# Sums of squares of the head outputs: added up per kind before TensorE sums them over partitions

## The reference, cut to what matters

```python
z = h @ w_in                         # q, k, v of both kinds, gate path, forget logits
o_sb = stick_breaking_attention(...) # (1024, 512)
o_fx = forgetting_attention(...)     # (1024, 512)
y = concatenate([rmsnorm(o_sb, g_grp[:512]), rmsnorm(o_fx, g_grp[512:])])   # one mean square per row and kind
y = y * silu(g_path)
x = x + (1 + gate) * (y @ w_out)
return rmsnorm(x, g_final)
```

## Time and profile before

| | before |
|---|---|
| median of 3 runs | 832.3 us (832.14 to 835.11) |
| profiled execution, first to last instruction | 828.7 us |
| around the span (median less span) | 3.6 us |
| mean granted TensorE clock | 0.973 |
| PE busy | 720.7 us (87%) |
| DVE busy | 490.9 us (59%) |
| ACT busy | 408.4 us (49%) |
| POOL busy | 390.7 us (47%) |

### The profile page before, as it was taken

The page is one execution under the profiler, slowest core; times in us unless marked ns, Lnnn a source line. Parts: engine busy times, 40 slices in busy tenths (PEclk is TensorE's granted clock), DMA queues, the critical chain, the costliest instruction groups (busy, mean ns, idle before and its releaser), DMA issues.

```text
span 828.7 us, 10998 instructions
## 1 busy us (share of the span) xinstructions
PE 720.7 (87%) x3936; PEld 604.4 (73%) x3936; DVE 490.9 (59%) x993; ACT 408.4 (49%) x846; POOL 390.7 (47%) x325
## 2 busy tenths in 40 slices
PE   0257965989999999999989989998899899999996
PEld 0146754768887887888777878887788788788884
DVE  1486663776564567756634676565447765545565
ACT  4027333576457555554645555555556465623132
POOL 2244422535866563467476644665556465221100
PEclk9988997999999999999989999999999999999998
DMA  6553332104245431133342411244432308894223
GB/s 185 183 200 148 129 100 40 35 22 86 98 102 138 108 103 26 26 91 102 88 136 57 102 26 26 77 128 127 152 94 67 85 25 304 243 311 166 68 90 128
DMA packets 64390, 91.57 MB, mean 111 GB/s; under 512 B 5448, under 2 KB 39880, under 8 KB 63824
## 3 DMA queue, kind: packets, MB, share of 16 engines
q1 hardware_dynamic: 57216, 72.17, 30.4%
q0 software_dynamic: 5376, 14.68, 5.6%
q10 hardware_dynamic: 1744, 4.02, 1.2%
HBM read 67.23 MB, written 23.63 MB: 110 GB/s over the span
## 4 chain that ended last, share of the span: by engine, by line
PE 34%; DMA 21%; POOL 19%; issue 9%; DVE 9%; ACT 6%; SPq 1%; DVEq 0%; POOLq 0%; ACTq 0%
DMA w_raw<-in_w_in 15%; PE psum L1376 10%; POOL w_lo L540 6%; DMA work<-in_w_ada_t 5%; PE psum L1290 4%; PE psum L1291 4%; PE psum L1295 4%; PE psum L1364 4%; DVE work L1037 3%; PE psum L1342 3%; POOL w_hi L534 3%; POOL work L554 2%; POOL work L608 2%; DVE stacks L1005 2%; POOL work L614 2%
## 5 line engine op out<-in xcount | busy, mean ns | idle before, releaser
L1290 PE MATMUL psum<-h_hi,w_hi 128*128 128x512 f32 x496 | 209.6, 423 | 23.9 <-POOL h_lo L591 13.5
L1295 PE MATMUL psum<-h_hi,w_lo 128*128 128x512 f32 x496 | 197.6, 398 | 0.0
L1291 PE MATMUL psum<-h_lo,w_hi 128*128 128x512 f32 x496 | 197.2, 398 | 0.0
L800 ACT ACTIVATE pt_hi<-psum 128x512 fp32r<-128x512 f32 (+1 forms) x192 | 87.5, 490 | 140.5 <-PE psum L1342 137.3
L1097 DVE TENSOR_TENSOR pt_lo<-psum,pt_hi 128x512 fp32r<-128x512 f32 (+1 forms) x192 | 100.6, 551 | 84.4 <-ACT pt_hi L800 83.4
L608 POOL TENSOR_TENSOR work<-work 128x127 f32<-128x127 f32 (+3 forms) x64 | 77.4, 1211 | 152.2 <-DVE work L1037 152.2
L1290 PEld LDWEIGHTS psum<-h_hi,w_hi 128*128 128x128 f32 x496 | 96.0, 193 | 43.6 <-issue 16.2
L1037 DVE TENSOR_TENSOR_SCAN work<-work 128x128 f32<-128x128 f32 (+3 forms) x64 | 104.1, 1627 | 32.5 <-ACT work L768 32.4
L1342 PE MATMUL psum<-ident,work 128*128 128x128 f32 x576 | 88.8, 282 | 29.9 <-POOL work L614 16.0
L1295 PEld LDWEIGHTS psum<-h_hi,w_lo 128*128 128x128 f32 x496 | 95.5, 192 | 22.2
L1291 PEld LDWEIGHTS psum<-h_lo,w_hi 128*128 128x128 f32 x496 | 96.1, 194 | 16.6
(11 more groups left out here) (141 smaller groups left out, 1291.5 us busy)
## 6 DMA issues: line engine op xcount, KB each, us to landing
w_raw<-in_w_in SPq DMA_DIRECT2D x32, 512.0 KB, 9.4
work<-in_w_ada_t SPq DMA_DIRECT2D x24, 512.0 KB, 9.2
work<-in_x SPq DMA_DIRECT2D x16, 512.0 KB, 6.6
w_split_scratch<-work SPq DMA_DIRECT2D x16, 512.0 KB, 3.4
y_split_scratch<-work SPq DMA_DIRECT2D x10, 512.0 KB, 3.7
work<-forget_scratch SPq DMA_DIRECT2D x8, 512.0 KB, 5.1
work<-in_w_out SPq DMA_DIRECT2D x16, 256.0 KB, 5.6
stacks<-y_split_scratch POOLq DMA_DIRECT2D x4, 1024.0 KB, 6.7
```

The source lines that it names most:

```text
L800: nc.scalar.activation(pt_hi[:, a:e, (g % 2) * P:(g % 2 + 1) * P], bank, ACT.Copy).then_inc(s_thi, 1)
L1290: nc.tensor.matmul(bank, hi, h_hi[:, c_, cols], start=(c_ == 0), stop=False)
L1291: last = nc.tensor.matmul(bank, hi, h_lo[:, c_, cols], start=False, stop=(kind == "f" and c_ == DC - 1))
L1295: last = nc.tensor.matmul(bank, lo, h_hi[:, c_, cols], start=False, stop=(c_ == DC - 1))
```

## The change

For the first seven pairs the square moves from POOL to ACT: in stage p+1, step 2, `square_pair` writes `O_T` squared into `sq_sum[kind]` for pairs 0 and 1, and into `VT` for pairs 2 to 6. POOL then adds `VT` to `sq_sum[kind]` in step 3 (`add_squares`, pairs 2 to 6). PE sums over partitions only in stage 7, step 4, once per kind (`sum_squares(5)` and `sum_squares(6)`), and once more for the last pair after the loop, as before. The square root and `inverse_root` of the stick-breaking kind come one step later (step 5). `O_T` may be overwritten once ACT has squared it and POOL has gated it. `sq_sum` takes 8 KB in each partition, and the launch line now sets the scratch space of dynamic DMAs to 4096 bytes.

```diff
-    def squares_step(p):
-        return 3 if p == PAIRS - 1 else 5
+    SUMS_AT = 4
+    def squares_added(p):
+        return max(0, p - 1)
...
-        if g == UNITS or p >= 1 and i == squares_step(p):
+        if g < UNITS and (p, i) == (PAIRS - 1, SUMS_AT):
+            t_items += [("SS", p - 2, 0), ("SS", p - 1, 0)]
+        if g == UNITS:
             t_items.append(("SS", p - 1, 0))
...
+        sq_sum = sb("sq_sum", [P, 2, SEQ])
...  SP
                 if n == 3:
-                    sp.wait_ge(s_tfree, T_ITEM["SS", LAST - 1, 0])
+                    sp.wait_ge(s_sq, squares_added(LAST - 1))
...  POOL
-            def square_pair(p):
-                pool.wait_ge(s_t, T_ITEM["V", p + 1, 1])
-                nc.gpsimd.tensor_tensor(VT, O_T, O_T, ALU.mult).then_inc(s_sq, 1)
+            def add_squares(p):
+                pool.wait_ge(s_sqa, p + 1)
+                nc.gpsimd.tensor_tensor(sq_sum[:, p % 2, :], sq_sum[:, p % 2, :], VT, ALU.add).then_inc(s_sq, 1)
...
-                if i == 1 and p >= 1:
-                    square_pair(p - 1)
+                if i == 3 and p >= 3:
+                    add_squares(p - 1)
...  ACT
-                    if p >= 2:
-                        act.wait_ge(s_tfree, T_ITEM["SS", p - 2, 0])
+                    if p >= 4:
+                        act.wait_ge(s_sq, squares_added(p - 2))
                     nc.scalar.activation(VT[:, cols], bank, ACT.Copy).then_inc(s_phi, 1)
...
+            def square_pair(p):
+                act.wait_ge(s_pvd, (p + 1) * STEPS // 2)
+                nc.scalar.activation(VT if p >= 2 else sq_sum[:, p, :], O_T, ACT.Square).then_inc(s_sqa, 1)
...
-                if p == LAST and i == squares_step(p) + 1:
+                if p == LAST and i == SUMS_AT + 1:
                     act.wait_ge(s_rv, 3)
                     nc.scalar.activation(rms_s[:, 0:TB], rms_v[:, 0:TB], ACT.Sqrt).then_inc(s_rs, 1)
...
                 if i == V_STEPS[1]:
                     vt_out(p, 1)
+                    if p >= 1:
+                        square_pair(p - 1)
...  DVE
                 if q % (STEPS // 2) == 0 and q > 0:
-                    dve.wait_ge(s_sq, q // (STEPS // 2))
+                    dve.wait_ge(s_sqa, q // (STEPS // 2))
+                    dve.wait_ge(s_y, q // (STEPS // 2))
...
-                if p >= 1 and i == squares_step(p):
+                if p == LAST and i == SUMS_AT:
+                    squares_out(p - 2)
                     squares_out(p - 1)
...  PE
             def sum_squares(p):
-                pe.wait_ge(s_sq, p + 1)
+                pe.wait_ge(s_sq, squares_added(p))
                 bank = next_bank(("SS", p, 0))
-                squares = SQUARES if p == LAST else VT
+                squares = SQUARES if p == LAST else sq_sum[:, p % 2, :]
...
-                if p >= 1 and i == squares_step(p):
+                if (p, i) == (LAST, SUMS_AT):
+                    sum_squares(p - 2)
                     sum_squares(p - 1)
                 transpose_probs(g)
...
-    nc = bacc.Bacc("TRN2", target_bir_lowering=False, num_devices=1)
+    nc = bacc.Bacc("TRN2", target_bir_lowering=False, num_devices=1, dynamic_dma_scratch_size=4096)
```

More of the change, by code:

```diff
@@ L274, in hybrid_trunk_kernel @@
         s_y = sem("s_y")
+        s_sqa = sem("s_sqa")
         s_sq = sem("s_sq")
@@ L505, in _ @@
             load_z(0)
-            sp.wait_ge(s_sq, PAIRS)
+            sp.wait_ge(s_sq, squares_added(LAST))
             sp.wait_ge(s_y, PAIRS)
@@ L1084, in squares_out @@
                 dve.wait_ge(s_t, n)
-                if p >= 2:
+                if p == LAST:
                     dve.wait_ge(s_tfree, T_ITEM["SS", p - 2, 0])
@@ L1173, in _ @@
                     values_out(g // 2 - 1)
-                if p >= 1 and i == squares_step(p):
+                if p == LAST and i == SUMS_AT:
+                    squares_out(p - 2)
                     squares_out(p - 1)
[L1176 to L1179, removed]
+                    dve.wait_ge(s_tfree, T_ITEM["SS", LAST - 1, 0])
+                    mean_square(rms_v[:, 0:TB], ss_o[:, 0:TB], N_TYPE)
+                if p == LAST and i == SUMS_AT + 1:
                     inverse_root(rms_y[:, 0:TB], rms_v[:, 0:TB], rms_s[:, 0:TB], rms_t[:, 0:TB], 3)
```

## The result

The changed kernel takes 835.9 us (median of 20 runs, 832.3 to 839.6), the kernel before 832.3 (20 runs, 830.7 to 835.9): ratio 1.0038, 95% interval 1.0026 to 1.005. The forecast was 822.3 us, its range 818 to 830. The changed kernel's profiled execution has a span of 832.6 us against 828.7.

What follows compares the result with a forecast made beforehand. PE, busy 720.7 of 828.7 us, and its waits were taken as the bound. Terms -10.5 - 2.4 + 2.2 = -10.7, kept at -10.0, gave span 818.7 and 822.3 us with 3.6 around it; range 818 to 830.

Steps and rivals of the forecast that it cites:

- PE's sums: Stages 1 to 6 each lose one sum over partitions of 1.75 us on PE, 10.5 us in all.
- rival A: The saving is lost in odd stages if their weight loads don't move up, 3 x 1.75 us; 830.0 us, chance 0.12.
- GpSimd's square: Odd stages: POOL's chain moves up 1.9 us and PE's 1.75, together 1.75 a stage, already counted.
- The scan: DVE's step 7 scan in stages 2, 4, 6 begins before POOL's split; 0.8 us each, 2.4 in all.
- The loop as a whole: Stages 1 to 6: PE's sums, -10.5 us, and the scan, -2.4, together -12.9.
- The beginning: Up to the first gate product, at the head of stage 1: the forecast sum had no term for it, 0.
- Stage 7: Both sums come in step 4, 3.5 us; less 0.8 saved and 0.5 covered, net +2.2 us.
- the wait for h_hi: A sign of being wrong: PE waits more than 1 us for h_hi or h_lo.
- Tables (C): ACT's squares between exponentials: 0 extra table loads taken, bound 2 x 1.28 us in each of four odd stages; C's chance 0.07.
- scratch (B): Rival: POOL's DMAs run short of scratch and wait for landings around stage 7, +16 us, 838 us; chance 0.06.

Runs made afterwards that it cites:

- a_pe6: Changed kernel plus six sums of 16 records on PE, one in step 5 of each of stages 1 to 6; ratio 1.0022 to the kernel before.
- the padded ones: Seven versions of the changed kernel with added one-column matmuls at PE's start or end, four with one sum in stage 6; stages 1 to 6 average 468.4 us.
- b_sqact: Kernel before with the squares on ACT in step 2 instead of GpSimd in step 1, every sum kept on PE; ratio 0.9921.
- a_pad32: Changed kernel with 32 one-column matmuls at PE's start and nothing else; ratio 0.9917 to the kernel before.
- a_pad: Changed kernel with 96 one-column matmuls at PE's start; ratio 0.9973 to the kernel before.
- a_mid: Changed kernel with one of stage 7's two sums moved to step 5 of stage 6; ratio 0.9948 to the kernel before.
- a_mid_pad32: Changed kernel with one sum moved from stage 7 to stage 6 and 32 one-column matmuls at PE's start; ratio 0.987, repeated 0.9886.
- a_again: Changed kernel run once more, on another chip; ratio 0.9998 to the kernel before.
- a_scratch8k: Changed kernel with dynamic DMA scratch of 8192 bytes instead of 4096, all buffers 4096 bytes higher; ratio 1.0005 to the kernel before.
- b_scratch4k: Kernel before with only dynamic DMA scratch set to 4096 bytes, every buffer 12288 bytes lower; ratio 0.9992.

## Why the prediction was wrong, step by step

- **PE's sums, -10.5.** Too large, by about a third. They bring 6.3 to 7.3 us under the fast beginning (a_pe6, one profile, against the padded ones). As far as single stages can be told apart, the odd ones, where rival A saw the loss, give 5.2 of 5.25; the loss is in the even ones, 2.1 of 5.25, and nothing in stage 6. (Stage 2, from gate product to gate product, is 75.9 us long and not the 84 that the prediction names; nothing in its sum uses that.)
- **GpSimd's square, no gain of its own.** Wrong, to the good. Its move alone takes stages 1 to 6 from 478.8 to 474.3, and the whole kernel to 0.9921. I had let PE's and GpSimd's savings cover one another in odd stages, and had the first weight load of stage 1 moving up by 1.9 us, which it did: 224.05 - 211.23 = 12.8 us behind the gate product in the earlier trace rows, 235.40 - 224.47 = 10.9 after.
- **The scan, -2.4.** Right in kind, its size not measured by itself. The move of the squares alone, with PE's sums kept, already brings the scan from 3.90 us to 3.14 (b_sqact, all three even stages). Scans of step 7 in stages 2 and 4 of the changed kernel (start, us), for 3.90 in the earlier trace rows:

```profile
324.07 2.44 DVE L1053 TENSOR_TENSOR_SCAN work<-work 128x1024 f32<-128x1024 f32 x1 [1.22 <-ACT work L777]
...
477.99 2.63 DVE L1053 TENSOR_TENSOR_SCAN work<-work 128x1024 f32<-128x1024 f32 x1 [1.22 <-ACT work L777]
```

  An add and this scan don't meet. The scan of step 6 does meet one, in stages 4 and 6, and takes 2.21 us there for 2.02 in stage 2, which has no add (add and scan of stage 4):

```profile
471.31 2.40 POOL L634 TENSOR_TENSOR sq_sum<-sq_sum,work 128x1024 f32<-128x1024 f32 x1
473.39 2.21 DVE L1053 TENSOR_TENSOR_SCAN work<-work 128x896 f32<-128x896 f32 x1 [1.00 <-ACT work L777]
```

  The rule on the shared port pair (the Trainium skill, "SBUF — State Buffer", "SBUF: two separate sides"), by which the instruction that starts first holds up the other, agrees in kind; the scan begins 0.3 us before the add's end and lost 0.2 us.
- **The loop as a whole, -12.9.** With the fast beginning it is 478.8 to 468.4, -10.4. So of the -13.8 measured, 3.4 us go with the long beginning and not with the change's work: the same loads land at other times (stage 3 alone is 78.7 us in the changed kernel and 83.4 in the mean of the padded ones, stage 2 is 1.7 us longer). That the loop came out near the forecast is in part luck.
- **The beginning, 0.** This is the step that failed. The sum went from stage 1 to the end and took all before it as fixed, because no instruction there is touched. It became 13.2 us longer: the first weight load landed in 14.9 us for 9.8, and PE's waits behind loads grew by 12 us in all. Why the loads are slower is open (below).
- **Stage 7, +2.2.** Mis-sized: +4.5. The two sums were priced at 1.75 us each, from a row at full clock; they took 6.73 us at half. Of the rest, the wait for h_hi is gone, as forecast.
- **Tables (C) and scratch (B).** 13 table loads as before; GpSimd's DMAs take 0.81 and 0.77 us to issue against 0.80 and 0.75, and the smaller scratch alone changed nothing (0.9992).

Without the long beginning, the changed kernel is what a_pad32 shows: 0.9917 (0.9890 to 0.9944), 6 to 7 us faster where 10 were forecast (a_pad, whose padding delays PE's first work, shows 0.9973). With the sum moved out of stage 7 alone (a_mid) it is 0.9948, the long beginning and all; with both edits (a_mid_pad32) it is 0.987 and 0.9886 on two chips, faster than both kernels. Against a_again and a_scratch8k, both level with before, the two edits are worth about 1.2%.

**What stays open.** Why the number of PE's instructions, or the length of the program, sets how fast the loads of x and of the weights move in the first microseconds and in stage 3. No engine's instruction differs there, and moving all buffers by 12 KiB doesn't matter. Nor was it tried to place the tensors elsewhere in the device's memory. Two rows of the page of the changed kernel are for the queues that bring instructions (transfers, MB, share):

```profile
q8 instruction: 31, 0.51, 0.2%
q14 instruction: 22, 0.18, 0.1%
```

The kernel before has 32 transfers on q8, but the number doesn't go with the pattern: a_pad32 has 31 and the fast beginning. The Trainium skill ("Runtime: NRT & Kernel Launch", section "Instruction fetch mechanics") has each sequencer fetch its instructions in blocks of 16 KiB by a DMA queue of its own, at a cost that is mostly hidden. The size agrees (0.51 MB in 31). That such transfers take their place among the data's doesn't explain the beginning: between the span's start and 60.5 us (before) or 71.2 us (changed) the trace has no transfer on either queue, and the data's rates part at 7 us. For the later loads it is open. Where the turn lies between 80 and 16 records fewer wasn't tried, nor was any other engine's count changed in a program that has the long beginning.

## What to carry to other kernels

Before a difference of a per cent is put down to an edit, cut both profiles at a mark that both have and look first at the stretches that the edit doesn't touch; if one of them moved, pad the program back to its old length with idle instructions, on the engine whose count changed and in a wait long enough to hide them, and compare again. Undoing one part changes the length too, so a part needs its own padded twin. Price a moved instruction at the granted clock of the place where it will stand, not of the place it comes from.

## What the runs showed of the hardware that was not expected

- The time from issue to landing of the same load, from the same line to the same buffer, is 9.2 to 9.9 us in 15 programs and 14.4 to 14.9 in the five that have 80 or 96 PE records of 3936 fewer (and with them the fewest instructions in all); from 9 to 12 us the DMAs move 341 to 412 GB/s or 27 to 80. A longer PE program (+192) gave yet another set in the loop (16.4 us for 13.3).
- Matmuls of one column took 0.11 us a record at full clock and 0.21 to 0.22 at a granted clock of 0.50 (16 in 3.58 us). At PE's very start, where the row of the granted clock says 1.00, they also took 0.21 (72 records in 15 us).
- In all twelve versions of the changed kernel the granted clock fell 1.4 to 4.4 us after the end of a PE wait of 1.7 us in stage 7. The kernel before and its versions show that the wait alone doesn't set it: the clock fell within the wait (before), ahead of it (b_sqact) or 8 us behind it (b_scratch4k).
